# Row writes of the first router on ScalarE's queue, and attention two steps behind its projections

## The reference, cut to what matters

```python
h = h + mlstm_mixer(rmsnorm(h, norm_mix[0]), ...)          # layer 0, 272 tokens
h = h + hier_moe(rmsnorm(h, norm_ffn[0]), ...)
k, v, F = shared_kv(h, kv_norm, kv_w, kv_b_f, k_norm)      # K, V and forget sums for layer 1
h = h[:, N_META:]
q = rmsnorm(_heads(h @ w_q, F_HEADS, F_HD), g_q) * (F_HD ** -0.5)
s = einsum('bhqd,bhkd->bhqk', q, k) + f_q[..., None] - F[:, :, None, :]
p = softmax(where(kpos <= qpos, s, NEG)); o = einsum('bhqk,bhkd->bhqd', p, v)
h = h + o @ w_o
h = h + hier_moe(rmsnorm(h, norm_ffn[1]), ...)             # layer 1, 256 tokens
```

## Time and profile before

| what | value |
|---|---|
| time, median of 3 runs | 592.33 us (591.47 to 594.24) |
| the profiled execution's own time | 591.58 us |
| its span, first to last instruction | 589.7 us |
| PE busy | 566.8 us, 96% of the span |
| DVE, ACT, POOL busy | 36%, 25%, 7% |
| mean granted clock of PE | 0.99 |

### The profile page before, as it was taken

One profiled execution on the slowest core, in us unless ns is written; L12 is line 12 of the kernel. 1 busy time (PEld: TensorE's weight loads), 2 busy tenths in 40 slices (PEclk: granted clock), 3 DMA queues, 4 the chain that ended last, 5 costly groups with the idle time before them and its releaser, 6 DMA issues.

```text
span 589.7 us, 9193 instructions
## 1 busy us (share of the span) xinstructions
PE 566.8 (96%) x3668; PEld 366.0 (62%) x3668; DVE 211.7 (36%) x617; ACT 146.9 (25%) x409; POOL 42.5 (7%) x92
## 2 busy tenths in 40 slices
PE   8999999999859999999999999999999999999997
PEld 4687878889744354444366777877799734333332
DVE  3353113331205574444364433444422246222222
ACT  3213113331203121111064233333322322111110
POOL 8000000000100120000001111111000011000000
PEclk9999999999969999999999999999999999999999
DMA  9979730030659799999999806040212999999992
GB/s 282 349 173 350 239 132 1 4 139 1 197 235 387 253 422 419 420 419 422 371 349 339 294 1 214 1 144 0 82 63 83 383 348 377 421 420 420 422 404 77
DMA packets 58648, 148.25 MB, mean 251 GB/s; under 512 B 10061, under 2 KB 42893, under 8 KB 46317
## 3 DMA queue, kind: packets, MB, share of 16 engines
q1 hardware_dynamic: 54112, 136.06, 62.2%
q0 software_dynamic: 3024, 10.95, 5.0%
q10 hardware_dynamic: 1468, 0.65, 0.5%
HBM read 144.41 MB, written 3.23 MB: 250 GB/s over the span
## 4 chain that ended last, share of the span: by engine, by line
PE 85%; DMA 9%; DVE 2%; ACT 1%; issue 1%; ACTq 0%; SPq 0%; DVEq 0%
PE bank L1549 29%; PE bank L1873 18%; PE bank L1684 9%; PE bank L1900 7%; DMA ring<-in_moe_w_up 5%; PE bank L1926 3%; PE bank L1929 2%; PE bank L1844 2%; DMA qk_area<-xs,idx 2%; PE bank L1653 2%; DMA xs<-big 1%; PE bank L2081 1%; PE bank L2066 1%; PE bank L2112 1%; PE bank L1828 1%; PE bank L2108 1%
## 5 line engine op out<-in xcount | busy, mean ns | idle before, releaser
L1549 PE MATMUL bank<-hxT,ring 128*128 128x272 f32 x576 | 138.2, 394 | 1.1 <-ACT hxT L890 0.6
L1549 PEld LDWEIGHTS bank<-hxT,ring 128*128 128x128 f32 x576 | 107.8, 190 | 23.4 <-issue 2.4
L1873 PE MATMUL bank<-ring,gate_area 128*64 128x512 f32 (+1 forms) x608 | 114.9, 595 | 1.0 <-DMA ring<-in_moe_w_up 1.0
L1873 PEld LDWEIGHTS bank<-ring,gate_area 128*64 128x64 f32 (+1 forms) x608 | 34.9, 125 | 57.0 <-issue 55.7
L1684 PE MATMUL bank<-tok,ring 128*128 128x128 f32 (+1 forms) x512 | 64.3, 283 | 0.1
L1684 PEld LDWEIGHTS bank<-tok,ring 128*128 128x128 f32 x512 | 61.4, 194 | 1.7 <-issue 1.5
L1900 PE MATMUL bank<-ring,gate_area 128*32 128x512 f32 x448 | 51.7, 595 | 0.0
L1228 DVE TENSOR_TENSOR qk_area<-qk_area,bank 128x256 f32<-128x256 f32 x16 | 6.7, 421 | 81.0 <-ACT qk_area L835 81.0
L1900 PEld LDWEIGHTS bank<-ring,gate_area 128*32 128x32 f32 x448 | 13.9, 109 | 32.8 <-issue 31.9
L835 ACT ACTIVATE qk_area<-bank 128x256 f32<-128x256 f32 x16 | 6.1, 384 | 100.6 <-PE bank L1873 100.6
L827 ACT ACTIVATE gate_area<-bank,gains_x 128x128 f32<-128x128 f32 x64 | 18.3, 368 | 50.8 <-PE bank L1844 45.6
(11 more groups left out here) (309 smaller groups left out, 649.2 us busy)
## 6 DMA issues: line engine op xcount, KB each, us to landing
ring<-in_moe_w_gate SPq DMA_DIRECT2D x30, 1024.0 KB, 13.3
ring<-in_moe_w_up SPq DMA_DIRECT2D x30, 1024.0 KB, 15.6
ring<-in_moe_w_down SPq DMA_DIRECT2D x28, 1024.0 KB, 18.6
ring<-in_m_w_in SPq DMA_DIRECT2D x11, 1024.0 KB, 12.8
ring<-in_kv_w SPq DMA_DIRECT2D x8, 1024.0 KB, 13.1
ring<-in_m_w_out SPq DMA_DIRECT2D x4, 1024.0 KB, 12.9
ring<-in_f_w_q SPq DMA_DIRECT2D x4, 1024.0 KB, 12.6
ring<-in_f_w_o SPq DMA_DIRECT2D x4, 1024.0 KB, 7.6
```

What stands on the lines that cost most here:

```text
L1549: ins = pe.matmul(bank[c % 2][:, 0:n], w[:, k, half * P:half * P + P], x[:, k, 0:n], start=(k == 0), stop=(k == KB - 1))
L1873: ins = pe.matmul(bank[1][s, :], xgT[b % 2][:, q, s], unit_gate_up(g, q), start=(q == 0), stop=(q == KB - 1))
```

## The change

Three edits. First, the DMA writes of tiles 0 and 1 of layer 0 are issued by ACT, each right behind the two ACT instructions that make the tile, and count on a semaphore of their own, `xs0_first`, for which POOL waits ahead of the first gather. The write of tile 2 stays on POOL, and `xs_written` counts it alone in layer 0. Second, attention handles pair a = j - 2 in step j, on PE, DVE and ACT, so that there are ten steps: step 1 has no attention, steps 8 and 9 no projections. Third, the blocks of the output projection are dealt anew over the last two steps: k = 0 to 5 for all eight blocks ahead of the transposes and values, k = 6 ahead of the last values, k = 7 at the end as before.

```diff
@@ POOL, moe(l) @@
                     for t, rows, c0 in part_tiles(l, p):
+                        if l == 0 and p == 0:
+                            continue
                         pool.wait_ge(*in_layer("rows_made", l, t + 1))
                         pool.dma_start(xs[l][c0 - off:c0 - off + rows, :], rows_home(l, t)).then_inc(sem("xs_written"), 16)
                     if l == 0 and p == 0:
-                        pool.wait_ge(sem("xs_written"), 32)
+                        pool.wait_ge(sem("xs0_first"), 32)
                         pool.wait_ge(sem("idx_ready"), 1)
@@ ACT, part_rows(p), behind the two activations of a tile @@
                         ins.then_inc(sem("rows_made"), 1)
+                        if l == 0 and p == 0:
+                            act.wait_ge(sem("rows_made"), t + 1)
+                            c = tiles[t][2]
+                            act.dma_start(xs[0][c:c + rows, :], rows_home(0, t)).then_inc(sem("xs0_first"), 16)
@@ ACT, DVE and PE, loop over the head pairs @@
-            for j in range(KB + 1):
-                a = j - 1
+            for j in range(KB + 2):
+                a = j - 2
@@ PE, fillers behind scores(a) @@
                 elif j == KB:
                     pe.wait_ge(*read("proj", "kqv1", 0, 12))
-                    for jo in range(4):
-                        out_block(1, 0, jo, 0, KB - 1)
+                    for jo in range(3):
+                        out_block(1, 0, jo, 0, KB - 2)
+                elif j > KB:
+                    for jo in (5, 6, 7):
+                        out_block(1, 0, jo, 0, KB - 2)
@@ PE, fillers behind probs_tr(a) @@
+                elif j == KB:
+                    out_block(1, 0, 3, 0, KB - 2)
+                    pe.wait_ge(*read("proj", "kqv1", 1, 12))
+                    out_block(1, 0, 4, 0, KB - 2)
                 else:
-                    pe.wait_ge(*read("proj", "kqv1", 1, 12))
-                    for jo in (4, 5):
-                        out_block(1, 0, jo, 0, KB - 1)
+                    for jo in range(KB):
+                        out_block(1, 0, jo, KB - 2, KB - 1)
@@ PE, behind the loop @@
-            for j in (6, 7):
-                out_block(1, 0, j, 0, KB - 1)
             pe.wait_ge(sem("o_read"), KB)
```

More of the change, by code:

```diff
@@ L300, in wait_bank @@
                 pe.wait_ge(*read(kind, ph, j % 2, j // 2))
-        LAYER0 = {"xs_written": 48, "rows_made": 3, "idx_ready": 3, "tx_done": 16, "ktot_ready": 1,
+        LAYER0 = {"xs_written": 16, "rows_made": 3, "idx_ready": 3, "tx_done": 16, "ktot_ready": 1,
                   "out_done": 7, "h_ready": 5, "sq_ffn": 5, "logits_mm": 2,
@@ L622, in moe @@
                             in_offset=bass.IndirectOffsetOnAxis(ap=idx[:, 0:1], axis=0)).then_inc(sem("x_in0"), 16)
-                pool.wait_ge(*in_layer("xs_written", l, 16 * len(tiles_of(l)[0])))
+                pool.wait_ge(*in_layer("xs_written", l, 16 * (1 + l)))
                 for b in range(2, NPAIR):
@@ L841, in y_evac @@
                     if b == 0:
-                        act.wait_ge(*in_layer("xs_written", l, 16 * nt))
+                        act.wait_ge(*in_layer("xs_written", l, 16 * (1 + l)))
                     if b == 1:
@@ L1242, in y_evac @@
                     if b == 0:
-                        dve.wait_ge(*in_layer("xs_written", l, 16 * nt))
+                        dve.wait_ge(*in_layer("xs_written", l, 16 * (1 + l)))
                     dve.tensor_copy(ybuf(b)[:, 0:HALF], bank[2][:, :]).then_inc(sem("y_read0"), 1)
```

## The result

| | median, us | range, us | runs |
|---|---|---|---|
| before | 593.5 | 591.39 to 595.16 | 20 |
| after | 594.81 | 592.45 to 597.04 | 20 |

The ratio is 1.0023 with a 95% interval of 1.0013 to 1.0033: the changed kernel is slower by 1.4 us (0.8 to 2.0). The forecast was 590.9 us, 2.6 under the median of before above, with a range to 593.8. The time lies outside it, on the other side.

The account below looks back on a forecast made before the run. PE, busy 96% of the span, was taken as the bound, its 9.4 us gather wait the main loss. Sum: 591.6 - 3.7 (writes) + 2.6 (attention) = 590.5; adding half of 0.75 gave 590.9 us, range 588.2 to 593.8.

Parts of the forecast that it names:

- Gain 3.7 us: Layer 0 row writes: issued by ACT, they land at 155.66, so the gather is issued at 155.94, not 159.64.
- come in behind tile 0's first packets, so 3.8: Row writes: SP's weights issued at 151.10 trail tile 0's packets, so the set takes 3.8 us, not 4.1.
- The slower rival: Row writes on ACT wait behind SP's queued weights; behind two loads they land at 163.2, giving 598.1 us; chance 0.07.
- nothing else of the gather changes, so I leave it its 9.27 us: First gather in layer 0: takes 9.27 us from its issue, as before.
- I count the whole 3.7: Behind the gather: later loads shift with PE, so all 3.7 us of the gain reach the end.
- the clock rises about 3 us behind PE's resuming: PE behind the gather wait: half clock lasts the same 3.1 us as before, though the wait is shorter.
- the low clock eats half the gain: Behind the gather: clock stays low to 172.1 us, so the writes bring 1.9 us, total 592.3; chance 0.17.
- The attention, +2.6: Attention with the lag: five uncovered waits less 0.4 us at the first softmax, +2.6 us, bounds 1.6 and 3.6.
- The three waits of step 1: Attention step 1: square sums of K +0.45 us, of Q +0.47, transposes of V +0.9, their covers lost.
- those for the copies of pairs 6 and 7: Attention step 9 and the end: PE waits for DVE's copies of the values, +0.6 us each.
- The faster rival, hidden waits in the steady steps: Attention steady steps: the lag removes waits hidden in PE's busy time, 2.8 us over six steps; chance 0.25.
- 589.1 and 589.2: Faster rival's totals: 589.1 us with half the hidden waits, 589.2 with the writes' upper bound of 5.0 us.

Follow-up runs that it names:

- pool_hold: Kernel before, row writes left on POOL, SP's weight load held until both row writes have landed: 590.16 us, 0.9944 of before.
- lag_only: Kernel before with only the lag of two steps and the new dealing of output blocks, writes on POOL: 596.0 us, 1.0057 of before.
- lag_mended: Lag alone, with covering products put back in step 1 and behind the last values: 592.97 us, 1.001 of before.
- lag_step1: Lag alone, with covering products put back in step 1 only, the end as in the change: 593.95 us, 1.0014 of before.
- write_hold: Kernel before with row writes on ACT and SP's weight load held until both have landed: 588.96 us, 0.9941 of before.
- gather_hold: Kernel before with row writes on ACT and SP's weight load held until the first gather has landed: 583.64 us, 0.9843 of before.
- issue_hold: As the kernel holding loads until the gather lands, but POOL releases SP's load by an increment behind the gather: 588.53 us, 0.9934 of before.
- gap_late: As the kernel holding loads until the gather lands, but PE releases SP's load behind step 42 of out_second: 583.21 us, 0.984 of before.
- gap_early: As the kernel holding loads until the gather lands, but PE releases SP's load behind step 35 of out_second: 581.12 us, 0.9804 of before.

## Why the prediction was wrong

**The row writes: the step that failed** is "Gain 3.7 us", by its reason that "the issue-to-packet time is what the two queues differ in". The 4.0 us behind POOL's issue in the earlier trace rows were read as a property of POOL's queue. With the load of weights held they are 1.36 us, on the same queue. The load was in the same group of rows (SP's at 151.10), and the prediction used it only as a mild neighbour: its weights "come in behind tile 0's first packets, so 3.8". That held for tile 0, not for tile 1. Shown: the gain of the writes is 1.4 us, and 3.4 us come from holding the load with the writes left where they were (pool_hold).

**The page of the skill.** The Trainium skill's page "DMA: Bandwidth & Descriptors", section "Latency and other measured facts", gives about 0.6 against about 1 us to the first byte. The prediction said that the trace disagreed. Once the load is away it agrees in the difference: 0.85 against 1.36 us here. The comparison of 0.9 and 4.0 had set a write with no load beside it against one with a load.

**The slower rival** ("served behind the weights that SP has in its queue") had the mechanism, at 0.07. Its size was off: tile 1's write waited behind one load, until 157.8, and did not wait for the second. Its own threshold, a landing at 156.8 or later, was crossed.

**"nothing else of the gather changes, so I leave it its 9.27 us"** was off by 0.5 us, and more was missed there. Of those 9.27 us about half was the same effect, loads ahead of the gather: without them the gather takes 4.3 us.

**"I count the whole 3.7"**, the gain kept. Of 1.1 us at PE's resuming, 0.26 is left at the first experts. The forecast that the clock rises about 3 us behind PE's resuming is wrong: it rose after 4.3 us or more. The 3.1 us of before was one execution's: in lag_only, lag_mended and lag_step1, whose layer 0 is that of before, the clock rose 4.8, 5.4 and 4.3 us behind PE's resuming. The rival "the low clock eats half the gain" described this, and here it ate more than half. That is read from one pair of traces; the writes alone, with 0.7 us left at the first experts in their trace, gave 1.4 us in the runs. Larger gains are mostly kept: in write_hold PE resumed 3.9 us sooner than before and the first experts began 3.0 us sooner, and in gather_hold, with no load beside the gather, the clock was not lowered at all.

**The attention, +2.6**: right in size and place. 2.82 us in the trace, 3.4 (2.4 to 4.3) in the runs. The three waits of step 1 are 0.5, 0.5 and 0.9 us, as forecast, those for the copies of pairs 6 and 7 0.6 and 0.5. The steady steps did not change. That the covers are the cause is shown by lag_mended, which puts them back and takes as long as before. Step 1 as a whole and the end were parted in the traces only (2.2 and 0.6 us), the single waits not at all. The faster rival, hidden waits in the steady steps at 0.25, came to nothing: they take 15.61 us as before. Its 589.1 and 589.2 also start from 590.5, without the 0.4 that the forecast of 590.9 adds.

**The start of the sum.** It stood on one execution and three runs, 1.2 us below what twenty runs gave. This alone would have moved the forecast to 592.1, still on the wrong side.

**Left open.** Where between 0.3 and 1.1 us behind the small transfer's issue a load stops doing harm was not measured, nor by what part of the hardware the load gets ahead. The traces suggest one rule that no run tests. With nothing else under way, the first packet came 1.0 us behind its issue for a load of SP (before, issue_hold, gap_late), 0.85 for ACT's write, 1.36 for POOL's and 1.8 to 1.9 for the gather. In every trace here the transfer whose first packet would come first by these figures went first, and the other was held up. In the kernel before, this was the load, by 0.1 us (152.07 against 150.78 + 1.36); in gap_early it was the gather, by 0.2 us (157.7 against 156.85 + 1.0), and there the load's first packet came only at 159.0. By this estimate a load would have to be issued 0.4 us or more behind a write of POOL's and 0.9 us or more behind a gather.

## What to carry to other kernels

When a small transfer on which everything waits shows microseconds without a packet, look first at what another queue issued just ahead of it or shortly behind it (0.3 us behind did harm here, 1.1 us did not), and hold that back; only then think about which engine issues it. A prefetch that has room may cost more by its moment than by its bytes: one wait on the engine that loads the weights gave 7.5 us here, where the move of the writes alone gave 1.4. A handoff that a steady loop hides for nothing must be paid at its first and last step when the loop is shifted, so fillers belong there.

## What the runs showed of the hardware

- A load of 1 MB issued on SP's queue 0.3 us behind a write on POOL's queue moved the write's first packet from 1.36 to 4.0 us behind its issue. Issued 0.2 to 0.3 us ahead of a gather, with more loads following within a microsecond, it moved the gather's from 1.9 to 4.5 us. Issued 0.6 us behind a write on ACT's queue, or 1.1 us behind the gather, it did not delay the start; nor did one issued 1.0 us behind ACT's second write delay its landing (3.08 against 3.06 us).
- The clock was granted at 0.50 for part of every PE wait for the gather of 4.4 us or more that was measured here, and around no wait for it of 1.7 us or less. In the changed kernel it was still 0.50 4.3 us behind the end of the wait. Apart from the first and last microseconds of a kernel it was lowered in one other place: in the trace of gap_early (582.96 us, the slowest of its five runs) it was 0.50 from 487.8 to 491.2 us, behind a wait of 1.0 us for weights in layer 1 that gap_late does not have at that place.
- A semaphore increment placed in POOL's program behind an indirect DMA took effect before that DMA's own record began: SP, which waited for it, issued 0.2 us ahead of the gather.
